# Six slots for the experts' weights, and the up product in two loops of six chunks

## The chip, the core and the metric

The kernel runs on one core of one Trainium2 chip. The metric is the device time of one execution in microseconds (us); lower is better. The core's engines are named as in the profile: PE (TensorE; PEld is its weight loads, PEldq its sequencer), DVE (VectorE), ACT (ScalarE), POOL (GpSimd) and SP (SyncE), which in this kernel issues nearly all transfers from HBM.

## The reference

`x` has 256 tokens of width 1024, in fp32. A first block of two layers (swiglu, a mixer with dilated attention and a short convolution, swiglu again) is followed by a second block: an mLSTM layer with a dense swiglu, then a state-space (S5) layer with a mixture of experts. The change touches this last part alone:

```python
def moe_ffn(u, w_router, w13, w2):
    t = u.reshape(-1, D)
    logits = t @ w_router
    top_val, top_idx = lax.top_k(logits, TOP_K)          # 2 of 8 experts
    top_w = jax.nn.softmax(top_val, axis=-1)
    for e in range(N_EXPERTS):
        gate_e = sum(where(top_idx == e, top_w, 0))
        out = out + gate_e[:, None] * swiglu(t, w13[e], w2[e])
```

`w13[e]` is 1024 x 5632 (gate and up side by side), `w2[e]` is 2816 x 1024, so an expert has 33,792 KB of weights. Each is read once.

## The kernel before

**Staging of weights.** Weights go from HBM through a ring of three slots in SBUF (`ring`, `SLOTS = 3`, 5632 fp32 columns each). SP runs through all chunks of the program in one fixed order. Before each it waits on the slot's semaphore `chunk_done`, which PE (or DVE) raises when it has finished with the slot, and the transfer raises `chunk_in`, on which PE waits (`chunk_landed`). The class `Place` works out, from a count of everything that comes earlier, which slot and which use of it a chunk has (`slot`, n % 3 and n // 3). Numbers that grow inside a hardware loop are computed in registers.

**The end of the state-space layer.** It is followed by the product `glu` (four chunks) and a layer norm, then the router: a product, the choice of two experts per token, ranks, and a count of tokens for each expert. In this stretch (2211 to 2232 us) PE, DVE and ACT hand small pieces to each other. The three slots are filled with the first chunks of expert 0 by then, and SP waits.

**The expert loop.** PE's code (`expert`, L1321) is a hardware loop over eight experts (L1379). In it `count` is loaded into a register, and an If (L1381) takes one of two bodies: `expert(e, NARROW)` where at most 88 tokens chose the expert, and, laid out behind it, `expert(e, S)` for up to 256. In the profiled execution all eight experts took the narrow body; at its end PE's sequencer jumps over the wide body to the two instructions that close the loop, and from there back to its start. A body has four steps:

- gather: the chosen tokens are picked by a product with a selection matrix (L1331, L1339); ACT and DVE copy them to `h`.
- up: `Rounds(4, (4, 4, 3), DT, "up_e")`. A hardware loop of four rounds on PE (`up_rounds`, L1298, its branch is L1303), each with three chunks of 4, 4 and 3 output tiles of 128 columns, 2048, 2048 and 1536 KB. That is 11 tiles x 8 steps of depth x 2 halves of the columns at L1314. The first two rounds are the gate's 22 tiles, which ACT takes through Silu into `mid` (L1831); the other two are the up's, which DVE multiplies into `mid` (L3068). ACT and DVE each have a hardware loop of two rounds for this. Four PSUM banks are used in turn, starting from bank 0 in each round.
- down: `Sides((0, 8, 15, 22), "down_e")`. Two halves of 512 output columns, each in three chunks of 8, 7 and 7 tiles of depth (2048, 1792 and 1792 KB), at L1358.
- scatter: the result is spread back to the tokens (L1374) and DVE adds it to `x`.

So an expert has 12 chunks of up and 6 of down, 18 in all, and each of the three slots is used six times.

**The work area.** `work` has 112 tiles of 256 columns. The experts use tiles 0 to 59 of it (`mid` 0 to 21, selections 24 to 29, the tokens `h_tok` 44 to 51, `y_pos` 52 to 59), the router's weights lie at 60, and `y_t` of `glu` at 96 to 103. The state-space layer uses nearly all of `work` until its last output has been moved (`gelu_moved`).

Of the kernel before, what the change touches and what calls it, by code (L numbers as in the profile page):

```python
# [15 lines left out]
P = 128  # L16
# [22 lines left out]
NE = 8  # L39
# [11 lines left out]

SLOTS = 3
WIDE = 2 * FT * P
BANKS = 8
# [64 lines left out]
class Rounds:  # L119
# [4 lines left out]
    def __init__(self, rounds, chunks, depth, source):  # L124
        self.rounds, self.depth, self.source = rounds, depth, source
        self.edges = [depth * sum(chunks[:c]) * P for c in range(len(chunks) + 1)]
        self.per_full, self.per_free = [0] * LIN, [0] * LIN
        self.at, n = [], 0
        for groups in chunks:
            row = []  # L130
            for m in range(groups):
                b = n % LIN
                row.append((n, b, self.per_full[b], self.per_free[b]))
                self.per_free[b] += 1
                if m < groups - 1:
                    self.per_full[b] += 1
                n += 1
            self.at.append(row)
        self.groups = n

    def counts(self):
        c = {"chunk": self.rounds * SLOTS, "of " + self.source: self.rounds}
        for b in range(LIN):
            c[f"full{b}"] = self.rounds * self.per_full[b]
            c[f"free{b}"] = self.rounds * self.per_free[b]
        return c


class Sides:
# [7 lines left out]
    def counts(self):  # L157
        return {"chunk": 2 * self.parts, "of " + self.source: 2, **{f"free{b}": 1 for b in range(LIN)}}

# [26 lines left out]
def stages():  # L186
# [90 lines left out]
class Place:  # L277


    def __init__(self, plan, name, rep=0):  # L280
        self.name, self.what, self.rep = name, plan.stage[name], rep
        self.base, self.period = plan.base[name], plan.period[name]

# [105 lines left out]
def build(nc, dram, out, periods):  # L389
    plan = Plan()  # L390
    with ExitStack() as ctx:
# [184 lines left out]
        bank_full = [signal[f"full{b}"] for b in range(BANKS)]  # L576
        chunk_in = [sem(f"chunk_in{s}") for s in range(SLOTS)]
        chunk_done = [sem(f"chunk_done{s}") for s in range(SLOTS)]
        small_in = sem("small_in")
# [46 lines left out]

        def round_end(p, c, m, i, after=0):

            n, b, k, _ = p.what.at[c][m]
            if m == len(p.what.at[c]) - 1:  # L630
                slot, use = p.slot(c, i)
                return chunk_done[slot], use + after + 2
            return bank_full[b], products(p, b, k + after * p.what.per_full[b], i, p.what.per_full[b])

# [5 lines left out]
        def _(sp):  # L640
# [20 lines left out]
            def stream_rounds(p):  # L661
                lin = p.what
                with sp.Fori(0, lin.rounds) as i:
                    src = dram[lin.source][p.of("of " + lin.source, 0, i, 1)]
                    for c, (lo, hi) in enumerate(zip(lin.edges, lin.edges[1:])):
                        slot, use = p.slot(c, i)
                        sp.wait_ge(chunk_done[slot], use + 1)
                        sp.dma_start(ring[:, slot, 0:hi - lo], src[:, lo:hi]).then_inc(chunk_in[slot], 16)

            def stream_sides(p):  # L670
                down = p.what
                for side in range(2):
                    src = dram[down.source][p.of("of " + down.source, side)]
                    for part, (lo, hi) in enumerate(zip(down.edges, down.edges[1:])):
                        slot, use = p.slot(side * down.parts + part)
                        sp.wait_ge(chunk_done[slot], use + 1)
                        sp.dma_start(ring[:, slot, 0:(hi - lo) * 512], src[:, lo * 512:hi * 512]).then_inc(chunk_in[slot], 16)

# [23 lines left out]
        def _(pe):  # L702
# [596 lines left out]
            def up_rounds(p, gp, width):  # L1299

                lin = p.what
                columns = columns_of_tile(width)
                with pe.Fori(0, lin.rounds) as i:  # L1303
                    for c, members in enumerate(lin.at):
                        slot = chunk_landed(p.slot(c, i))
                        for m, (n, b, _, k_free) in enumerate(members):
                            pe.wait_ge(bank_free[b], reads(p, b, k_free, i, lin.per_free[b]))
                            for k in range(lin.depth):
                                if c == 0 and m == 0:
                                    fb, use = gathered(k)  # L1310
                                    pe.wait_ge(bank_free[fb], reads(gp, fb, use) + 1)
                                w = ring[:, slot, (m * lin.depth + k) * P:(m * lin.depth + k + 1) * P]
                                for lo, hi in columns:
                                    mm = pe.matmul(half(b)[lo:hi, 0:width], w[:, lo:hi], h[:, k, 0:width],  # L1314
                                                   start=(k == 0), stop=(k == lin.depth - 1))
                            if m == len(members) - 1:
                                mm.then_inc(chunk_done[slot], 1)
                            else:
                                mm.then_inc(bank_full[b], 1)

            def expert(e, width):  # L1321
# [28 lines left out]
                for side in range(2):  # L1350
                    for part, (first, last) in enumerate(zip(down.edges, down.edges[1:])):
                        slot = chunk_landed(p.slot(side * down.parts + part))
                        if side == 0 and part == down.parts - 1:
                            for _, b, _, _ in late:
                                pe.wait_ge(bank_free[b], reads(p, b))
                        for n in reversed(range(lists)):
                            for k in range(first, last):
                                mm = pe.matmul(bank(2 * side + n)[0:slots(n), :],  # L1358
                                               mid[:, k, n * P:n * P + slots(n)],
                                               ring[:, slot, (k - first) * 512:(k - first + 1) * 512],  # L1360
                                               start=(k == 0), stop=(k == FT - 1))
# [37 lines left out]
        def _(act):  # L1399
# [419 lines left out]
            for e in steps.loop("expert", NE):  # L1819
# [6 lines left out]
                lin = p.what  # L1826
                with act.Fori(0, lin.rounds // 2) as i:
                    for c, members in enumerate(lin.at):
                        for m, (n, b, _, k) in enumerate(members):
                            act.wait_ge(*round_end(p, c, m, i))  # L1830
                            act.activation(mid[:, at(i, lin.groups, n), :], half(b), ACT.Silu).then_inc(bank_free[b], 1)  # L1831
                p = place("downE", e)
                for side in range(2):
                    slot, use = p.slot((side + 1) * p.what.parts - 1)
                    act.wait_ge(chunk_done[slot], use + 2)
# [12 lines left out]
        def _(dve):  # L1848
# [1201 lines left out]
            def one_expert(e, between=None):  # L3050
# [255 lines left out]
```

## Time and profile before

| | us |
|---|---|
| median of three runs | 3071.79 (3070.0 to 3074.74) |
| the profiled execution's own time | 3076.41 |
| its span in the trace | 3074.3 |
| experts, start of expert 0's products to the end of expert 7 | 2232 to 3054 |
| share of TensorE's full clock, mean | 0.991 |

The page of the profile sums each engine's busy time and idle time over the span; the rows by stretch and the timeline say where they lie. "Idle before" an instruction is put down to what released it; "issue" means that nothing the profile shows was waited for. Records of PE come in two kinds, MATMUL (PE) and LDWEIGHTS (PEld); each fp32 product has two of either. The profile's DMA part lists transfers by queue: q1 carries the weights that SP asks for, q8 carries instructions.

### The profile page before, as it was taken

To read this page: it belongs to the slowest core of one execution; us is meant where nothing else is said; L and a number is where in the kernel's file an instruction comes from. 1 tells how busy PE (TensorE), PEld (TensorE's weight loads), DVE (VectorE), ACT (ScalarE), POOL (GpSimd) and SP (SyncE) were. 2 spreads that over 40 slices of the span, in tenths; PEclk is the share of its full clock that TensorE was granted. 3 is DMA by queue.
4 is the path that set the end of the run, shared out by engine and by line. 5 is a ranking of instruction groups with operands and counts; after the bars stand their busy time and mean duration, and the time that the engine had idled before them with its cause. 6 is when DMAs were issued, how large, how long until landed. Compare 5 with 4: busy or idle time off the path is not lost.

```text
span 3074.3 us, 68427 instructions
## 1 busy us (share of the span) xinstructions
PE 2939.0 (96%) x28798; PEld 2585.7 (84%) x28799; DVE 1586.9 (52%) x3012; ACT 608.9 (20%) x1439; POOL 15.6 (1%) x27
## 2 busy tenths in 40 slices
PE   5999999999999999999999989997999999999999
PEld 4999888899999989889999779986786668766875
DVE  6776662376677667326767458899421112111212
ACT  1111104121111211412112302135212101210121
POOL 0000000000000000000000000000000000000000
PEclk9999999999999999999999999998999999999999
DMA  7665654355466565534556347832287898889885
GB/s 306 255 248 192 260 216 188 137 193 206 193 250 243 220 246 220 199 113 190 213 213 233 127 180 301 322 145 83 105 328 296 315 368 344 328 317 368 344 330 202
DMA packets 55543, 733.17 MB, mean 238 GB/s; under 512 B 6608, under 2 KB 6792, under 8 KB 10804
## 3 DMA queue, kind: packets, MB, share of 16 engines
q1 hardware_dynamic: 51364, 716.68, 59.9%
q0 software_dynamic: 3984, 13.74, 1.3%
q8 instruction: 140, 2.29, 0.3%
q14 instruction: 55, 0.45, 0.0%
HBM read 729.31 MB, written 4.23 MB: 239 GB/s over the span
## 4 chain that ended last, share of the span: by engine, by line
PE 82%; DMA 11%; DVE 5%; issue 1%; ACT 1%; SPq 0%; DVEq 0%; ACTq 0%
PE psum L728 35%; PE psum L819 17%; PE psum L1358 10%; PE psum L1314 9%; DMA ring<-in_up_e_dram 4%; PE psum L806 3%; PE psum L722 2%; DMA ring<-in_up_dram 2%; DMA ring<-in_down_e_dram 1%; PE psum L1374 1%; DMA ring<-in_w_v_dram 1%; DVE ring L1866 1%; DMA ring<-in_w_ccch_dram 1%; PE psum L1339 1%; DMA ring<-in_ada_dram 1%
## 5 line engine op out<-in xcount | busy, mean ns | idle before, releaser
L1314 PE MATMUL psum<-h_t,ring 128*64 128x88 f32 x11264 | 436.5, 239 | 16.5 <-DMA ring<-in_up_e_dram 16.1
L1314 PEld LDWEIGHTS psum<-h_t,ring 128*64 128x64 f32 x11264 | 430.2, 137 | 22.2 <-issue 21.1
L728 PE MATMUL psum<-work,ring 128*128 128x128 f32 x3680 | 440.8, 275 | 2.2 <-ACT work L1447 2.2
L728 PEld LDWEIGHTS psum<-work,ring 128*128 128x128 f32 x3680 | 425.2, 192 | 3.1 <-issue 1.6
L728 PE MATMUL psum<-work 128*128 128x128 f32 x3328 | 388.9, 275 | 2.0 <-issue 1.0
L728 PEld LDWEIGHTS psum<-work 128*128 128x128 f32 x3328 | 380.0, 192 | 2.6 <-issue 2.0
L1866 DVE SCALAR_TENSOR_TENSOR ring<-ring,cond 128x1024 f32<-128x1024 f32 x240 | 279.3, 1219 | 86.7 <-DMA ring<-in_ada_dram 86.6
L1358 PE MATMUL psum<-ring,work 128*88 128x512 f32 x704 | 304.0, 593 | 2.4 <-DMA ring<-in_down_e_dram 2.4
L819 PE MATMUL psum<-work,ring 128*128 128x256 f32 x1344 | 296.2, 383 | 4.8 <-DMA ring<-in_m_out_dram 3.1
L819 PEld LDWEIGHTS psum<-work,ring 128*128 128x128 f32 x1344 | 257.4, 192 | 42.2 <-DMA ring<-in_m_out_dram 3.9
L819 PE MATMUL psum<-h_t,ring 128*128 128x256 f32 x1280 | 278.8, 380 | 1.0 <-ACT h_t L1568 1.0
L819 PEld LDWEIGHTS psum<-h_t,ring 128*128 128x128 f32 x1280 | 242.4, 190 | 36.0 <-issue 2.8
L1358 PEld LDWEIGHTS psum<-ring,work 128*88 128x88 f32 x704 | 109.9, 157 | 190.9 <-issue 187.3
L728 PE MATMUL psum<-h_t,ring 128*128 128x128 f32 x2272 | 266.3, 275 | 4.3 <-DMA ring<-in_up_dram 3.3
L728 PEld LDWEIGHTS psum<-h_t,ring 128*128 128x128 f32 x2272 | 259.9, 192 | 6.9 <-DMA ring<-in_up_dram 4.4
L3068 DVE TENSOR_TENSOR work<-work,psum 128x256 f32 x176 | 74.1, 421 | 369.0 <-PE psum L1314 369.0
L1958 DVE TENSOR_TENSOR work<-ring 128x1024 f32<-128x1024 f32 (+1 forms) x93 | 120.0, 1291 | 144.7 <-DMA ring<-in_up_dram 77.4
L3074 DVE SCALAR_TENSOR_TENSOR x_t<-psum,mod,x_t 128x256 f32<-128x256 f32 x64 | 28.0, 483 | 293.9 <-PE psum L1374 293.9
L728 PE MATMUL psum<-h_t,work 128*128 128x128 f32 x1136 | 138.4, 275 | 0.0
L728 PEld LDWEIGHTS psum<-h_t,work 128*128 128x128 f32 x1136 | 132.6, 192 | 0.0
L806 PE MATMUL psum<-work,ring 128*128 128x257 f32 x448 | 102.9, 388 | 29.7 <-DVE work L2202 26.0
L806 PEld LDWEIGHTS psum<-work,ring 128*128 128x128 f32 x448 | 86.4, 194 | 44.8 <-issue 31.7
(378 smaller groups left out, 2538.8 us busy)
## 6 DMA issues: line engine op xcount, KB each, us to landing
ring<-in_up_e_dram SPq DMA_DIRECT2D x64, 2048.0 KB, 8.3
ring<-in_ada_dram SPq DMA_DIRECT2D x60, 2048.0 KB, 8.0
ring<-in_up_dram SPq DMA_DIRECT2D x55, 2048.0 KB, 8.7
ring<-in_down_e_dram SPq DMA_DIRECT2D x32, 1792.0 KB, 8.1
ring<-in_down_dram SPq DMA_DIRECT2D x20, 2816.0 KB, 10.3
ring<-in_up_e_dram SPq DMA_DIRECT2D x32, 1536.0 KB, 8.9
ring<-in_down_e_dram SPq DMA_DIRECT2D x16, 2048.0 KB, 8.3
ring<-in_w_qk_dram SPq DMA_DIRECT2D x12, 2048.0 KB, 8.2
```

The costliest lines, as they stand in the source:

```text
L722: mm = pe.matmul(half(bank_of), right(i), left(0, i), start=(first and i == 0), stop=(i == lin.depth - 1), skip_group_check=not first)
L728: mm = pe.matmul(bank(bank_of)[:, pair * P:(pair + 1) * P], w, right(i), start=(first and pair == 0 and i == 0), stop=(pair == lin.pairs - ...
L806: mm = pe.matmul(psum[:, b * 512:b * 512 + S + 1], ring[:, slot, (m * DT + k) * P:(m * DT + k + 1) * P], raw[:, k, :], start=(k == 0), sto ...
L819: mm = pe.matmul(half(b), w, moving(k, j * lin.groups + m), start=(k == 0), stop=(k == depth - 1))
L1314: mm = pe.matmul(half(b)[lo:hi, 0:width], w[:, lo:hi], h[:, k, 0:width], start=(k == 0), stop=(k == lin.depth - 1))
L1339: mm = pe.matmul(half(b)[lo:hi, 0:width], h_tok[:, t, f * P + lo:f * P + hi], sel[:, t, 0:width], start=(t == 0), stop=(t == TT - 1))
L1358: mm = pe.matmul(bank(2 * side + n)[0:slots(n), :], mid[:, k, n * P:n * P + slots(n)], ring[:, slot, (k - first) * 512:(k - first + 1) * 512],
L1374: mm = pe.matmul(half(b), y_pos[0:slots(n), n, f * P:(f + 1) * P], gate_sel[0:slots(n), n, :], start=(n == 0), stop=(n == lists - 1))
L1866: e = dve.scalar_tensor_tensor(w, w, 1.0, cond[:, :], ALU.mult, ALU.mult, accum_out=col)
L1958: dve.tensor_tensor(s1, a21, a22, ALU.add).then_inc(signal["weight_sums"], 1)
L3068: dve.tensor_tensor(o, o, half(b), ALU.mult).then_inc(bank_free[b], 1)
L3074: dve.scalar_tensor_tensor(x[:, f, :], half(b), mod1[:, 5 * DT + f:5 * DT + f + 1], x[:, f, :], ALU.mult, ALU.add).then_inc(bank_free[b], 1)
```

## The change

`DEEP` is 6. Slots 0 to 2 remain the ring's, slots 3 to 5 are three stretches of the work area, tiles 60 to 107. Only the experts' chunks go round all six (`deep`), so each slot is used three times in an expert. SP's order is unchanged: glu's four chunks, then expert 0's. SP may fill slots 3 to 5 for the first time when DVE has raised their `chunk_done`, which it does right after `gelu_moved`. To make room, `y_t` moves to tiles 36 to 43 and the router's weights to 108. A round of up now has six chunks, (4, 4, 3, 4, 4, 3), and there are two rounds: the first is the whole gate, the second the whole up. PE keeps a hardware loop, now over two rounds with a body of 22 tiles, in the narrow and in the wide body alike. ACT's and DVE's loops over rounds are gone; their 22 instructions stand one behind the other. SP computes the source's address for each chunk and not once for a round.

```diff
 SLOTS = 3
+DEEP = 2 * SLOTS
...
-        self.edges = [depth * sum(chunks[:c]) * P for c in range(len(chunks) + 1)]
+        self.per_row = len(chunks) // 2
+        starts = [sum(chunks[c - c % self.per_row:c]) for c in range(len(chunks))]
+        self.edges = [(c // self.per_row, depth * n * P, depth * (n + many) * P) for c, (n, many) in enumerate(zip(starts, chunks))]
...
-        "upE": Rounds(4, (4, 4, 3), DT, "up_e"), "downE": Sides((0, 8, 15, 22), "down_e"),
+        "upE": Rounds(2, (4, 4, 3, 4, 4, 3), DT, "up_e"), "downE": Sides((0, 8, 15, 22), "down_e"),
...
+    def deep(self, pos, i=0):
+
+        pos += DEEP * 2 if self.name == "downE" else 0
+        n = self.plan.base["upE"]["chunk"] + pos % DEEP
+        slot, use = (n % SLOTS, n // SLOTS) if pos % DEEP < SLOTS else (pos % DEEP, 0)
+        use += pos // DEEP
+        for reg, per in ((self.rep, SLOTS), (i, 1)):
+            if isinstance(reg, int):
+                use = use + reg * per
+            else:
+                use = reg * per + use
+        return slot, use
...
-        y_t = tiles(96, DT)
+        y_t = tiles(36, DT)
...
-        w_router = flat(60, 1)[:, 0:DT * NE].rearrange("p (k n) -> p k n", n=NE)
+        w_router = flat(108, 1)[:, 0:DT * NE].rearrange("p (k n) -> p k n", n=NE)
+
+        deep_slot = [ring[:, n, :] for n in range(SLOTS)] + [flat(60 + 16 * n, 16) for n in range(SLOTS)]
...
                 with sp.Fori(0, lin.rounds) as i:
-                    src = dram[lin.source][p.of("of " + lin.source, 0, i, 1)]
-                    for c, (lo, hi) in enumerate(zip(lin.edges, lin.edges[1:])):
-                        slot, use = p.slot(c, i)
+                    for c, (part, lo, hi) in enumerate(lin.edges):
+                        src = dram[lin.source][p.of("of " + lin.source, part, i, 2)]
+                        slot, use = p.deep(c, i)
                         sp.wait_ge(chunk_done[slot], use + 1)
-                        sp.dma_start(ring[:, slot, 0:hi - lo], src[:, lo:hi]).then_inc(chunk_in[slot], 16)
+                        sp.dma_start(deep_slot[slot][:, 0:hi - lo], src[:, lo:hi]).then_inc(chunk_in[slot], 16)
...
                 with pe.Fori(0, lin.rounds) as i:
                     for c, members in enumerate(lin.at):
-                        slot = chunk_landed(p.slot(c, i))
+                        slot = chunk_landed(p.deep(c, i))
...
-                                w = ring[:, slot, (m * lin.depth + k) * P:(m * lin.depth + k + 1) * P]
+                                w = deep_slot[slot][:, (m * lin.depth + k) * P:(m * lin.depth + k + 1) * P]
...
-                with act.Fori(0, lin.rounds // 2) as i:
-                    for c, members in enumerate(lin.at):
-                        for m, (n, b, _, k) in enumerate(members):
-                            act.wait_ge(*round_end(p, c, m, i))
-                            act.activation(mid[:, at(i, lin.groups, n), :], half(b), ACT.Silu).then_inc(bank_free[b], 1)
+                for c, members in enumerate(lin.at):
+                    for m, (n, b, _, k) in enumerate(members):
+                        act.wait_ge(*round_end(p, c, m, 0))
+                        act.activation(mid[:, n, :], half(b), ACT.Silu).then_inc(bank_free[b], 1)
...
             dve.sem_inc(signal["gelu_moved"], 1)
+            for slot in range(SLOTS, DEEP):
+                dve.sem_inc(chunk_done[slot], 1)
...
-                for i in steps.loop("upE rounds", lin.rounds // 2):
-                    for c, members in enumerate(lin.at):
-                        for m, (n, b, _, k) in enumerate(members):
-                            dve.wait_ge(*round_end(p, c, m, i, lin.rounds // 2))
-                            o = mid[:, at(i, lin.groups, n), :]
-                            dve.tensor_tensor(o, o, half(b), ALU.mult).then_inc(bank_free[b], 1)
+                for c, members in enumerate(lin.at):
+                    for m, (n, b, _, k) in enumerate(members):
+                        dve.wait_ge(*round_end(p, c, m, 1))
+                        dve.tensor_tensor(mid[:, n, :], mid[:, n, :], half(b), ALU.mult).then_inc(bank_free[b], 1)
```

## Rows read from the trace of the kernel before

**Rows 1.** The page, part 1: busy time, share of the span, instructions.
```profile
PE 2939.0 (96%) x28798; PEld 2585.7 (84%) x28799; DVE 1586.9 (52%) x3012; ACT 608.9 (20%) x1439; POOL 15.6 (1%) x27
```

**Rows 2.** Busy time by stretch, experts 0 to 2 (columns in the first line).
```profile
core 0: us, PE busy (x) PEld busy (x) DVE busy (x) ACT busy (x) POOL busy (x), PEclk, DMA share, GB/s
...
2232.00:2333.20 101.20, 98.68 (x1577) 72.97 (x1576) 21.16 (x55) 15.80 (x33) 0.00 (x0) 1.00 0.85 334
2333.20:2442.30 109.10, 100.71 (x1579) 75.06 (x1578) 16.49 (x41) 15.78 (x33) 0.00 (x0) 0.97 0.80 318
2442.30:2544.40 102.10, 98.95 (x1578) 73.24 (x1578) 16.45 (x41) 15.79 (x33) 0.00 (x0) 1.00 0.86 339
```

**Rows 3.** Waits from 2232 to 3054 us: us in total, times, longest.
```profile
PE psum L1314 <- DMA ring<-in_up_e_dram: 16.1, 24, 1.3
...
PE psum L1358 <- DMA ring<-in_down_e_dram: 2.4, 5, 0.8
```

**Rows 4.** DMA from 2232 to 2333 us: GB/s in 40 slices, then issues.
```profile
GB/s 0 6 0 149 428 383 428 384 446 409 409 324 441 409 440 326 422 389 402 436 378 425 372 406 403 414 128 318 422 290 437 177 380 267 182 428 324 337 389 248
...
ring<-in_up_e_dram SPq DMA_DIRECT2D x8, 2048.0 KB, 8.5
```

**Rows 5.** Timeline of PE, 2248 to 2284 us: start, us, what, idle before.
```profile
2263.18 13.57 PE L1314 MATMUL psum<-h_t,ring 128*64 128x88 f32 x352 [0.40 <-DMA ring<-in_up_e_dram]
```

**Rows 6.** DMA queues by packets, 2210 to 2232 us: packets, MB, share.
```profile
q8 instruction: 2, 0.03, 0.5%
```

**Rows 7.** DMA queues, 2232 to 2345 us.
```profile
q8 instruction: 6, 0.10, 0.4%
```

**Rows 8.** DMA queues, 2333 to 2345 us, from the end of expert 0 on.
```profile
q8 instruction: 2, 0.03, 0.9%
```

**Rows 9.** DMA queues, 2345 to 3050 us: q1, with the line that follows it.
```profile
q1 hardware_dynamic: 17712, 236.46, 85.2%
issues: line engine op xcount, KB each, median us to landing
```

**Rows 10.** DMA queues, 820 to 1600 us, the second pass of the layer loop.
```profile
q8 instruction: 48, 0.79, 0.4%
```

**Rows 11.** The page, part 3: the same queue over the whole execution.
```profile
q8 instruction: 140, 2.29, 0.3%
```

**Rows 12.** Busy time by stretch, 820 to 1600 us (columns as in rows 2).
```profile
820.00:1600.00 780.00, 771.29 (x5854) 732.16 (x5853) 482.35 (x852) 149.57 (x401) 3.22 (x4) 1.00 0.55 208
```

**Rows 13.** Branches of PE's sequencer, line 1381: ns min/median/max.
```profile
L1381 PEldq COMPARE_BRANCH  x16: 76/129/5902, 2230.8 to 3052.7; - x16
```

**Rows 14.** The same, line 964, the layer loop's branch.
```profile
L964 PEldq COMPARE_BRANCH  x2: 82/1864/3646, 812.7 to 1589.4; - x2
```

**Rows 15.** The same, line 1303, the loop of up.
```profile
L1303 PEldq COMPARE_BRANCH  x32: 76/208/257, 2247.2 to 3011.7; - x32
```

**Rows 16.** The same, line 1379, the loop of experts.
```profile
L1379 PEldq COMPARE_BRANCH  x8: 76/208/238, 2338.2 to 3053.0; - x8
```

**Rows 17.** The page, part 5: groups of up and down.
```profile
L1314 PE MATMUL psum<-h_t,ring 128*64 128x88 f32 x11264 | 436.5, 239 | 16.5 <-DMA ring<-in_up_e_dram 16.1
...
L1358 PE MATMUL psum<-ring,work 128*88 128x512 f32 x704 | 304.0, 593 | 2.4 <-DMA ring<-in_down_e_dram 2.4
...
L3068 DVE TENSOR_TENSOR work<-work,psum 128x256 f32 x176 | 74.1, 421 | 369.0 <-PE psum L1314 369.0
```

**Rows 18.** Line 1339, and what it does.
```profile
L1339 PE MATMUL psum<-work x512: 239/239/409, 2231.9 to 2955.4; 128*64 128x88 f32 x171
```

**Rows 19.** Line 1374.
```profile
L1374 PE MATMUL psum<-work x128: 377/379/382, 2329.6 to 3053.5; 88*128 88x256 f32 x128
```

**Rows 20.** Timeline of PE around 2339 us.
```profile
2339.61 0.68 PE L1331 MATMUL psum<-ident,work 128*128 128x128 f32 x2 [6.41 <-issue]
```

**Rows 21.** Timeline of PE around 2443 us.
```profile
2442.88 0.43 PE L1331 MATMUL psum<-ident,work 128*128 128x128 f32 x2 [0.60 <-issue]
```

**Rows 22.** The chain of waits, 2232 to 2250 us: start, us, what.
```profile
2234.58 13.50 PE psum L1314 x352
```

More of the change, by code:

```diff
@@ L141, in counts @@
     def counts(self):
-        c = {"chunk": self.rounds * SLOTS, "of " + self.source: self.rounds}
+        c = {"chunk": self.rounds * SLOTS, "of " + self.source: 2 * self.rounds}
         for b in range(LIN):
@@ L157, in counts @@
     def counts(self):
-        return {"chunk": 2 * self.parts, "of " + self.source: 2, **{f"free{b}": 1 for b in range(LIN)}}
+        return {"chunk": SLOTS, "of " + self.source: 2, **{f"free{b}": 1 for b in range(LIN)}}
 class Made:
@@ L281, in __init__ @@
         self.name, self.what, self.rep = name, plan.stage[name], rep
[L282 removed]
+        self.plan, self.base, self.period = plan, plan.base[name], plan.period[name]
     def of(self, signal, k=0, i=0, per=0):
@@ L576, in build @@
         bank_full = [signal[f"full{b}"] for b in range(BANKS)]
-        chunk_in = [sem(f"chunk_in{s}") for s in range(SLOTS)]
-        chunk_done = [sem(f"chunk_done{s}") for s in range(SLOTS)]
+        chunk_in = [sem(f"chunk_in{s}") for s in range(DEEP)]
+        chunk_done = [sem(f"chunk_done{s}") for s in range(DEEP)]
         small_in = sem("small_in")
@@ L619, in group_end, with round_end @@
             return bank_full[b], products(p, b, k, i, 0 if isinstance(i, int) else p.what.per_full[b])
-        def round_end(p, c, m, i, after=0):
+        def round_end(p, c, m, i):
             n, b, k, _ = p.what.at[c][m]
             if m == len(p.what.at[c]) - 1:
-                slot, use = p.slot(c, i)
-                return chunk_done[slot], use + after + 2
-            return bank_full[b], products(p, b, k + after * p.what.per_full[b], i, p.what.per_full[b])
+                slot, use = p.deep(c, i)
+                return chunk_done[slot], use + 2
+            return bank_full[b], products(p, b, k, i, p.what.per_full[b])
         def gathered(f):
@@ L674, in stream_sides @@
                     for part, (lo, hi) in enumerate(zip(down.edges, down.edges[1:])):
-                        slot, use = p.slot(side * down.parts + part)
+                        slot, use = p.deep(side * down.parts + part)
                         sp.wait_ge(chunk_done[slot], use + 1)
-                        sp.dma_start(ring[:, slot, 0:(hi - lo) * 512], src[:, lo * 512:hi * 512]).then_inc(chunk_in[slot], 16)
+                        sp.dma_start(deep_slot[slot][:, 0:(hi - lo) * 512], src[:, lo * 512:hi * 512]).then_inc(chunk_in[slot], 16)
             for part, times in stages():
@@ L1351, in expert @@
                     for part, (first, last) in enumerate(zip(down.edges, down.edges[1:])):
-                        slot = chunk_landed(p.slot(side * down.parts + part))
+                        slot = chunk_landed(p.deep(side * down.parts + part))
                         if side == 0 and part == down.parts - 1:
@@ L1359, in expert @@
                                                mid[:, k, n * P:n * P + slots(n)],
-                                               ring[:, slot, (k - first) * 512:(k - first + 1) * 512],
+                                               deep_slot[slot][:, (k - first) * 512:(k - first + 1) * 512],
                                                start=(k == 0), stop=(k == FT - 1))
@@ L1826, in _ @@
                 lin = p.what
-                with act.Fori(0, lin.rounds // 2) as i:
-                    for c, members in enumerate(lin.at):
-                        for m, (n, b, _, k) in enumerate(members):
-                            act.wait_ge(*round_end(p, c, m, i))
-                            act.activation(mid[:, at(i, lin.groups, n), :], half(b), ACT.Silu).then_inc(bank_free[b], 1)
+                for c, members in enumerate(lin.at):
+                    for m, (n, b, _, k) in enumerate(members):
+                        act.wait_ge(*round_end(p, c, m, 0))
+                        act.activation(mid[:, n, :], half(b), ACT.Silu).then_inc(bank_free[b], 1)
                 p = place("downE", e)
                 for side in range(2):
-                    slot, use = p.slot((side + 1) * p.what.parts - 1)
+                    slot, use = p.deep((side + 1) * p.what.parts - 1)
                     act.wait_ge(chunk_done[slot], use + 2)
```

2 lines of the change are left out of this document (1 added, 1 removed).

## The prediction

> **What bounds the kernel now.** I read the page's first part, then busy time by stretch, then what PE waits for among the experts, and last the queue that carries instructions. PE is busy for 2939.0 us of 3074.3 [rows 1]; the change can only give back its idle time. An expert takes 102.1 us, of which PE is busy 98.95 [rows 2]. Of the idle time among all experts, 16.1 us in 24 waits is PE at up waiting for a chunk, and 2.4 us in 5 waits at down [rows 3]; each is short. One stands in the timeline: 0.40 us of idle before a round of 13.57 us [rows 5]. The rate is near what the transfers reach: the slices show 324 to 448 GB/s through up [rows 4], where a round asks for 5632 KB in 13.57 us, or 425 GB/s [rows 5].
>
> The row that matters more is another. q8 carries instructions, in packets of 16 KB (0.79 MB in 48) [rows 10]. Two packets come in the 21 us ahead of the experts, six in the 113 us of expert 0 and the start of expert 1 [rows 6, 7], and in the 705 us after that none: behind q1's line the list of queues ends [rows 9]. So PE's sequencer holds the code of the narrow body, and runs it seven times without a fetch. In the second pass of the layer loop every instruction has been run before, and yet 48 packets come [rows 10]: code of that length isn't held.
>
> How much code is a packet? The second pass has 5854 + 5853 records of PE and PEld [rows 12]; over 48 that is 244 to a packet, the rest being waits and register steps. A trip through the narrow body: one round of up 11264 / 32 = 352 products and as many loads [rows 17] (PE and PEld have equal counts [rows 1]), 704; down 88 and 88 [rows 17]; gather 64 and 64 [rows 18], and 4 of the transposes [rows 20]; scatter 16 and 16 [rows 19]. Together 1044, or 4.3 packets.
>
> What does it cost when code isn't there? PE's jump at L1381 over the wide body takes 5902 ns the first time, and 129 at the median [rows 13]. PE stood idle for 6.41 us [rows 20], where the next expert shows 0.60 [rows 21]. The layer loop's jump back, also to code not held, takes 3646 ns [rows 14], in a part of the kernel whose transfers average 208 GB/s [rows 12] and not 339 [rows 2]. Jumps to code that is held take 208 ns at the median, back to the start of a round or of an expert [rows 15, 16].
>
> **The change part by part.** The sum is made against the profiled execution's 3076.4 us (span 3074.3); the median shown is 4.6 us lower.
>
> *Waits for chunks.* With six slots a chunk is asked for up to five chunks ahead of its use. The mean demand, 339 GB/s [rows 2], stays below the 380 to 448 that most slices show [rows 4], and down takes 304 / 8 = 38 us [rows 17] for a third of the bytes, in which six slots fill up. All 18.5 us go: -18.5 (bounds: -18.5 and 0).
>
> *First loads.* Slots 3 to 5 are filled in the router stretch, where SP waits today and q1 is idle but for its first microseconds; nothing there waits for a large transfer. 0. It is hidden behind small pieces of DVE and PE; without that cover three chunks would take some 15 us (6 MB at the rates of rows 4).
>
> *ACT, DVE, SP.* ACT and DVE are busy some 16 us of an expert's 102 [rows 2]; a loop less changes nothing. Six address computations on SP lie ahead of transfers that are early. The banks' order has a wait at down for the tile before the last, which DVE has by then multiplied: it takes 0.42 us [rows 17], while the last tile's products take 13.57 / 11 = 1.2. 0, and at most 0.5 us for an expert if DVE were late, 4 us in all.
>
> *PE's code.* Up's body doubles: 1044 + 704 = 1748 records, 7.2 packets. The wide body behind it grows too, so the code that closes the expert loop lies farther off. One trip now touches eight packets of the body; the fetch runs one ahead (the jump at the end of expert 0 brings two packets, not one [rows 8]), so nine; with the two at the jump's target, eleven. Before, the same count gave eight (two and six [rows 6, 7]), and eight were held. Nothing shows that more are. What is held lies between 8 and 47 packets; I take the nearest row, eight. If the oldest go first, a round of eleven through a store of eight finds none of its next ones: both jumps of each expert miss, and all packets come again.
>
> The Trainium skill, in "Runtime: NRT & Kernel Launch", section "Instruction fetch mechanics", gives TensorE an instruction memory of 128 KiB, refilled in blocks of 16 KiB; that is eight blocks, and the block's size agrees with q8's packets here. The same section also says that only two blocks are a window and that a jump outside them stalls. By that, 32 jumps back to the start of a round of 2.9 packets would have missed in this trace; their median of 208 ns speaks against it [rows 15]. The measurement decides: more than two are held.
>
> Costs of the misses, each counted less the 0.2 us of a jump that hits:
> - The jump over the wide body: expert 0 pays it today; seven more. It comes while the last chunks of the refill are running, as today: 7 x 5.7 = +40 (low 7 x 3.4 = 24, if it meets quiet queues).
> - The jump back to the loop's start, missed seven times. It follows the first by 6 us, when six slots are full and transfers have ended, as at the layer loop: 7 x 3.4 = +24 (high 7 x 5.7 = 40).
> - Straight code at up's pace: 704 records in 13.5 us is 52 per us, so a packet lasts 4.7 us. In expert 0 the first round ran at that pace from fresh code in 13.50 us against 13.57 for a held one [rows 5, 22], so it cost nothing, but transfers had barely begun (0, 6, 0 and 149 GB/s in the first four slices [rows 4]). Under full traffic a fetch can take the 5.9 us of the jump, 1.2 us too long. Six such packets in seven experts: 0 to 50 us. I take 3 us for an expert, +21.
> - Up's own jump back stays a hit: its body is 1408 / 244 = 5.8 packets, seven blocks at most, one ahead is eight. It is made once for an expert where it was made three times; PE's queue covers it (13.57 us for a round, jump included). 0.
>
> Sum: -18.5 + 40 + 24 + 21 = +66.5, so 3142.9 for such an execution and **3138 us** against the median. With the low ends +29.5, 3101; with the high ends -18.5 + 40 + 40 + 50 = +111.5, 3183. PE ends up bound by its own fetches; what is late next is nothing, since chunks will be waiting.
>
> **The rivals.**
> - *The code fits.* The store holds eleven packets or more. For it: no row shows its upper end short of 48. Against it: nothing but the missing row. Then only the 18.5 us go: 3053. It decides at eleven packets held. This is the case on the other side.
> - *Up's jump back misses too*, if one of the eight is given up for the fetch ahead. Then each expert has one more miss and streams up's body twice: 8 x (3.4 + 3) = 51 more, 3189; to 3205 with dear misses.
> - *The deeper ring doesn't do what it says*: the code fits and PE waits on as before because the rate itself, 425 GB/s asked in up, is the limit. Against it: the mean demand. 3072.
>
> **How the numbers follow.** What this kernel's measurement can tell from no change is 0.2%, 6 us. The forecast 0.78, the code fits 0.10, up's jump misses as well 0.08, no gain and no loss 0.04. The forecast's own range is 3101 to 3183; with the second rival's and some slack at both ends, 3092 to 3205, which leaves out the two cases without misses and little more. Faster: 0.11, from the first rival and a part of the third. Slower: 0.86. The same: 0.03.
>
> **What would show it.** PE's waits for chunks under 2 us in all. At L1381 nine of sixteen jumps or so hit and eight take 3 to 6 us; at L1379 seven of eight take over 3 us; at L1303 all stay at 0.2. Nine to eleven packets on q8 for each expert, so 140 [rows 11] grows to some 220. Experts of 109 to 115 us, with 8 to 10 us of idle time at the transposes of L1331. If instead q8 shows 145 packets and experts take 100 us, the store was larger and I am wrong on the sign. If L1381 stalls but L1379 doesn't, the oldest aren't the first to go.

## The result, and the profile after

The changed kernel takes 3155.5 us (median of 4 runs, 3152.1 to 3157.8) against 3073.3 us for the kernel before (four runs by now, 3070.0 to 3074.9). The ratio is 1.0268, with a 95% interval of 1.025 to 1.0286: 82 us slower, where 66 were forecast. The profiled executions are 3152.1 and 3076.4 us, 76 us apart, and it is these that the views compare.

The page of the changed kernel, parts 1, 3 and 5, answers to [rows 1, 11, 17]. Up is now L1332.

```profile
PE 2947.8 (94%) x28798; PEld 2597.1 (82%) x28799; DVE 1586.7 (50%) x3012; ACT 600.4 (19%) x1431; POOL 15.6 (0%) x27
...
q8 instruction: 211, 3.46, 0.4%
...
L1332 PE MATMUL psum<-h_t,work 128*64 128x88 f32 x5632 | 223.4, 239 | 20.7 <-issue 20.7
```

PE's busy time is up by 9 us, its span by 76. q8 went from 140 packets [rows 11] to 211. The largest group of up has 20.7 us of idle time ahead of it, put down to "issue" and no longer to a transfer. By stretch, experts 0, 1 and 2, against [rows 2]:

```profile
2226.80:2328.00 101.20, 98.30 (x1577) 73.08 (x1576) 21.19 (x55) 14.73 (x32) 0.00 (x0) 1.00 0.86 335
2328.00:2441.40 113.40, 100.49 (x1578) 74.85 (x1578) 16.41 (x41) 14.74 (x32) 0.00 (x0) 0.95 0.78 307
2441.40:2554.50 113.10, 99.97 (x1578) 74.50 (x1578) 16.90 (x42) 14.74 (x32) 0.00 (x0) 0.95 0.79 312
```

Expert 0 takes 101.2 us in both kernels. From expert 1 on an expert takes 113 us and not 102. The third column from the end is the granted clock: 0.95 of full speed where it was 1.00. What PE waits for among the experts (L1349 is the transposes with which an expert begins, L1332 up, L875 the layer norm after the last expert), against [rows 3]:

```profile
PE psum L1349 <- issue: 74.5, 7, 10.9
...
PE psum L1332 <- issue: 20.7, 20, 2.1
...
PE psum L875 <- issue: 2.6, 1, 2.6
```

No wait for a chunk is left. In the place of 18.5 us of them stand 74.5 us ahead of the transposes of experts 1 to 7 and 20.7 us within up (2.9 of these in expert 0, which saves about as much in waits for chunks). In the kernel before, the wait ahead of the transposes (L1331) was:

```profile
PE psum L1331 <- issue: 9.8, 7, 6.4
```

The branches of PE's sequencer show what the 74.5 are. A miss is from here on a jump to code that isn't held, a hit one to code that is. First the jump over the wide body (L1399, before [rows 13]):

```profile
L1399 PEldq COMPARE_BRANCH  x16: 80/1685/5941, 2225.6 to 3124.1; - x16
```

The line has two branches for each expert, one that enters the body and is cheap, one that leaves it. Eight of the sixteen are slow, seven between 5.6 and 5.9 us and the last 3.3. The branch back to the start of the loop of experts (L1397, before [rows 16]), of which seven are taken:

```profile
L1397 PEldq COMPARE_BRANCH  x8: 79/4580/4951, 2333.0 to 3127.6; - x8
```

and up's own branch (L1321, before [rows 15]), which never misses:

```profile
L1321 PEldq COMPARE_BRANCH  x16: 76/156/256, 2258.9 to 3083.1; - x16
```

The chain of waits over the start of expert 1, start and duration in us, before [rows 20, 21]:

```profile
2327.98 10.74 issue
2338.72 0.68 PE psum L1349 x2
2339.41 4.04 PE psum L1357 x64
2343.45 16.07 PE psum L1332 x422
2359.52 0.55 issue
...
2365.13 0.87 issue
...
2371.07 0.74 issue
```

After 10.74 us of nothing the transposes and the gather run slower than before: 0.68 and 4.04 us against 0.43 and 2.58 for a gather at full clock. The granted clock was at 1.2 and not 2.4 GHz by then, as this stretch of the busy times shows (0.50). It begins 4.2 us into the pause and ends 3.7 us into the work:

```profile
2332.20:2342.40 10.20, 3.68 (x44) 3.35 (x46) 0.82 (x2) 0.77 (x2) 0.00 (x0) 0.50 0.03 5
```

Then, in the first pass over up's body, three pauses of 0.5 to 0.9 us. The second pass (28.18 us, 734 records) has none. Transfers on q8 in one expert (2441 to 2554 us), where the kernel before shows none [rows 9]:

```profile
q1 hardware_dynamic: 2637, 35.16, 78.5%
q8 instruction: 10, 0.16, 0.7%
```

Summed over the experts, from the first gather product to the end of the last scatter, the trace has 898.4 us against 821.9, 76.5 more: idle time at the transposes 74.5 - 9.8 = +64.7 (6.4 of the 9.8 are the one slow jump of before [rows 20]), pauses in up +20.5, waits for chunks -18.5, gather products 32.4 - 22.5 = +9.9 and transposes +1.5 at the lower clock. That is 78.1; 1.6 us of it are not placed. Behind the experts the last jump costs 2.6 us more, and the layer norm that follows it 1.7 us, again at the lower clock (its first products in the chain of waits, start and duration). Before:

```profile
3053.87 3.47 PE psum L857 x16
```

and after:

```profile
3127.88 5.19 PE psum L875 x16
```

Together that is 80.8 us. The part ahead of the experts happened to be 5.1 us shorter in this execution, which leaves the 76 of the spans.

### The profile page after: what moved, and what is told of

The parts are those of the page before. It is cut to its first block, busy times and chain, and to the rows that moved or that the text cites. A ratio compares the mean times of both kernels' runs of the same rounds, so it can differ in the third digit from the quotient of the medians.

```text
span 3150.1 us, 67796 instructions
## 1 busy us (share of the span) xinstructions
PE 2947.8 (94%) x28798; PEld 2597.1 (82%) x28799; DVE 1586.7 (50%) x3012; ACT 600.4 (19%) x1431; POOL 15.6 (0%) x27
## 4 chain that ended last, share of the span: by engine, by line
PE 86%; DVE 5%; DMA 5%; issue 4%; ACT 1%; SPq 0%; DVEq 0%; ACTq 0%
PE psum L746 34%; PE psum L837 17%; PE psum L1332 14%; PE psum L1376 10%; PE psum L824 3%; PE psum L740 2%; DMA ring<-in_up_dram 1%; DMA ring<-in_w_ccch_dram 1%; PE psum L1357 1%; PE psum L1392 1%; DVE ring L1883 1%; DMA ring<-in_ada_dram 1%; DMA ring<-in_m_out_dram 1%; PE psum L939 1%; DVE work L1869 1%
## 5 line engine op out<-in xcount | busy, mean ns | idle before, releaser
L746 PEld LDWEIGHTS psum<-work,ring 128*128 128x128 f32 x3680 | 425.2, 192 | 3.1 <-issue 1.6
L837 PEld LDWEIGHTS psum<-work,ring 128*128 128x128 f32 x1344 | 256.2, 191 | 43.1 <-DMA ring<-in_m_out_dram 5.1
L3085 DVE TENSOR_TENSOR work<-work,psum 128x256 f32<-128x256 f32 x176 | 74.1, 421 | 371.3 <-PE psum L1332 371.3
L1332 PE MATMUL psum<-h_t,work 128*64 128x88 f32 x5632 | 223.4, 239 | 20.7 <-issue 20.7
L1332 PEld LDWEIGHTS psum<-h_t,work 128*64 128x64 f32 x5632 | 218.0, 137 | 24.5 <-issue 24.5
L1332 PE MATMUL psum<-h_t,ring 128*64 128x88 f32 x5632 | 217.2, 239 | 0.0
L1332 PEld LDWEIGHTS psum<-h_t,ring 128*64 128x64 f32 x5632 | 215.2, 137 | 0.1
L1376 PE MATMUL psum<-ring,work 128*88 128x512 f32 x352 | 152.9, 594 | 0.0
L1376 PE MATMUL psum<-work 128*88 128x512 f32 x352 | 152.4, 592 | 0.0
L1376 PEld LDWEIGHTS psum<-work 128*88 128x88 f32 x352 | 55.3, 157 | 95.8 <-issue 95.8
## 6 DMA issues: line engine op xcount, KB each, us to landing
ring<-in_down_dram SPq DMA_DIRECT2D x20, 2816.0 KB, 10.5
work<-in_down_e_dram SPq DMA_DIRECT2D x16, 1792.0 KB, 10.2
```

The costliest lines, as they stand in the source:

```text
L746: mm = pe.matmul(bank(bank_of)[:, pair * P:(pair + 1) * P], w, right(i), start=(first and pair == 0 and i == 0), stop=(pair == lin.pairs - ...
L837: mm = pe.matmul(half(b), w, moving(k, j * lin.groups + m), start=(k == 0), stop=(k == depth - 1))
L1376: mm = pe.matmul(bank(2 * side + n)[0:slots(n), :], mid[:, k, n * P:n * P + slots(n)], deep_slot[slot][:, (k - first) * 512:(k - first + 1 ...
L3085: dve.tensor_tensor(mid[:, n, :], mid[:, n, :], half(b), ALU.mult).then_inc(bank_free[b], 1)
```

## The experiments

**e1: the longer code alone.** The kernel before, three slots, with PE's loop of up over pairs of rounds:

```diff
-                with pe.Fori(0, lin.rounds) as i:
-                    for c, members in enumerate(lin.at):
+                with pe.Fori(0, lin.rounds // 2) as pair:
+                    for i, c, members in [(at(pair, 2, r), c, members) for r in range(2) for c, members in enumerate(lin.at)]:
```

> The kernel before with its three slots and its chunks, but PE's loop of up written as two passes over a body of two rounds (22 tiles), narrow and wide. Only PE's code is longer; nothing of the six slots is in it. Theory (PE's sequencer holds eight packets of code, the oldest go first): the misses of the changed kernel are all there, the jump at the end of the narrow body over 5 us and the jump back to the loop's start over 4 us in each expert, q8 near 211 packets; waits for chunks stay in part, as three slots still run dry in up. 3155 to 3174 us. Rival (the loss comes from the slots in the work area or from SP's other order): no misses, 142 packets on q8, 3070 to 3076 us.

3192.3 us (3185.0 to 3194.6), ratio 1.0389 (1.0374 to 1.0405), 214 packets on q8. Waits of PE among the experts, then one expert's stretch:

```profile
PE psum L1331 <- issue: 74.2, 7, 10.9
...
PE psum L1314 <- issue: 21.0, 20, 2.0
PE psum L1314 <- DMA ring<-in_up_e_dram: 15.0, 16, 2.1
...
PE psum L1358 <- DMA ring<-in_down_e_dram: 3.9, 4, 1.9
```

```profile
2452.70:2570.00 117.30, 102.08 (x1580) 75.70 (x1578) 16.59 (x42) 15.79 (x33) 0.00 (x0) 0.94 0.77 297
```

The misses and the pauses are the changed kernel's to within 0.3 us, without one of its slots. So the code is what costs, and the slots gain: the changed kernel is 37 us faster than this one. My range ended at 3174. 18.9 us of the 37 are the waits for chunks that are left, which I had thought half hidden. PE's busy time among the experts is 9 us longer too (102.1 us in the expert shown against 100.0); a part of that is the clock (0.94 against 0.95), the rest is not placed.

**e2: no wide body.** The changed kernel, with its loop of experts cut to the narrow body:

```diff
-                many = pe.value_load(count[0:1, bass.ds(e, 1)], min_val=0, max_val=S)
-                with pe.If(many <= NARROW):
-                    expert(e, NARROW)
-                with pe.Else():
-                    expert(e, S)
+                expert(e, NARROW)
```

> The changed kernel without its wide body, and without the load of the count and the If (no expert has more than 88 tokens with these inputs). The narrow body is as long as in the changed kernel and ends in the eighth packet, but the two instructions that close the loop now stand right behind it. Theory: the long jump forward is gone with its 5.7 us for each expert; the fetch that runs ahead brings a ninth packet, so the jump back still misses (about 5 us) and all code comes again. 3155 - 7 x 6 = 3113, range 3100 to 3125, some 200 packets on q8. Rival (any body that doesn't change place, once it has been run, is held; only the far jump evicts): all hits, 3050 to 3060. Second rival (the length doesn't matter, the loss is in the slots): 3150 or more.

3086.2 us (3078.4 to 3096.3), ratio 1.0050 (1.0034 to 1.0066), 167 packets: faster than I said. The only branch left, back to the start of the loop:

```profile
L1397 PEldq COMPARE_BRANCH  x8: 78/222/6962, 2335.2 to 3054.7; - x8
```

Three of the seven miss, at 6.3 to 7.0 us: those after experts 1, 3 and 5. Experts 1, 2 and 3 by stretch, and q8 in the first two of them:

```profile
2335.50:2433.20 97.70, 97.70 (x1579) 72.97 (x1578) 16.30 (x40) 14.70 (x32) 0.00 (x0) 1.00 0.89 354
2433.20:2541.50 108.30, 100.21 (x1580) 74.55 (x1579) 16.45 (x41) 14.70 (x32) 0.00 (x0) 0.97 0.82 321
2541.50:2639.40 97.90, 97.90 (x1580) 73.12 (x1579) 16.50 (x42) 14.70 (x32) 0.00 (x0) 1.00 0.88 354
```

```profile
q1 hardware_dynamic: 2590, 34.58, 88.5%
q14 instruction: 1, 0.01, 0.0%
issues: line engine op xcount, KB each, median us to landing
```

```profile
q1 hardware_dynamic: 2591, 34.59, 81.2%
q8 instruction: 9, 0.15, 0.5%
```

Expert 1 fetches nothing and is over in 97.7 us; then the jump misses, expert 2 fetches its whole code again and takes 108; expert 3 is held again. Neither theory had this. A miss at the jump means that the start of the loop was put out for a ninth packet. The count bears that out: each miss comes with nine packets, the eight of the body and one just ahead of them, and 140 + 3 x 9 = 167; a hit brings none. Why the ninth was asked for only every second time, e10 takes up.

**e3: 96 instructions less.** As e2, and

```diff
-                        for lo, hi in columns_of_tile(width):
+                        for lo, hi in ((0, P),):
...
-                                for lo, hi in columns:
+                                for lo, hi in columns if n < lin.groups - 1 else ((0, P),):
```

> The kernel of e2 with 96 instructions less on PE, some 5% of the narrow body: the gather products and the last tile of up are made with all 128 columns in one product and not in two halves. The body then ends in the seventh packet, and with the one ahead eight are touched. Theory (eight packets held): no miss at all after expert 0, 145 packets or fewer on q8, experts of 99.5 to 100.5 us, 3052 to 3060 us, 55 us below e2. Rival (what is held is fewer than eight, or not decided by a count of packets): the jump back still misses, 3100 to 3125.

3059.4 us (3056.0 to 3066.7), ratio 0.9957 (0.9940 to 0.9973). The branch back, and q8 on the page:

```profile
L1397 PEldq COMPARE_BRANCH  x8: 67/209/231, 2334.8 to 3035.8; - x8
```

```profile
q8 instruction: 140, 2.29, 0.3%
```

No branch misses, and q8 is back at 140. An expert takes 100.1 us. A twentieth less code turns three misses into none. It is 27 us below e2 where 55 were expected, as e2 itself missed less. The shorter code isn't free: e2's experts whose code was held take 97.8 us.

**e4: six slots with the short code.** From the changed kernel: `"upE": Rounds(4, (2, 2, 2, 2, 2, 1), DT, "up_e")`, six chunks in a round of 11 tiles, and in `deep` the counts that go with it:

```diff
-        pos += DEEP * 2 if self.name == "downE" else 0
+        rounds = self.plan.stage["upE"].rounds
+        pos += DEEP * rounds if self.name == "downE" else 0
...
-        for reg, per in ((self.rep, SLOTS), (i, 1)):
+        for reg, per in ((self.rep, rounds + 1), (i, 1)):
```

ACT and DVE take their two rounds each one behind the other, without a loop.

> Six slots as in the changed kernel, wide body and If kept, but up in four rounds of 11 tiles on PE again, each round in six chunks of 2, 2, 2, 2, 2 and 1 tiles (1024 KB, the last 512), so that a chunk's slot is fixed in the code and PE's code is as long as before the change (one instruction more). Theory: the code is held as before, 141 to 144 packets on q8, and with five chunks of 1 MB asked for ahead PE's waits for chunks fall from 18.5 us to under 6: 3055 to 3062 us. Rival (small transfers cost more than they hide, or six slots don't help): 3068 to 3080. The code theory fails if it is over 3100.

**3050.1 us** (3044.9 to 3051.6), ratio 0.9920 (0.9907 to 0.9934): the fastest of all, 24 us under the kernel before, 105 under the changed one and 5 under my range, and it keeps the wide body. Experts 2 and 3, the branch at the end of the body, q8:

```profile
2434.00:2533.00 99.00, 98.41 (x1580) 73.25 (x1579) 16.54 (x41) 14.71 (x32) 0.00 (x0) 1.00 0.86 350
2533.00:2632.00 99.00, 98.42 (x1580) 73.15 (x1579) 16.55 (x42) 14.70 (x32) 0.00 (x0) 1.00 0.86 350
```

```profile
L1401 PEldq COMPARE_BRANCH  x16: 76/126/3802, 2230.2 to 3026.6; - x16
```

```profile
q8 instruction: 140, 2.29, 0.3%
```

One slow branch, as before the change; PE busy for 98.4 of 99.0 us; no wait for a chunk.

**e5: the small chunks with three slots.** The kernel before with e4's chunks, each slot used twice in a round.

> The kernel before with its three slots, but a round of up in six chunks of 2, 2, 2, 2, 2 and 1 tiles, as in e4. It parts the two things that e4 changes, slots and the chunks' size. If six slots make e4's gain: three slots then hold 3 MB and not 5.6, only 2 MB are asked for ahead, and PE waits more for chunks than the 18.5 us before: 3085 to 3130 us. If the chunks' size makes it: 3050 to 3060. No misses either way (one instruction more on PE than before, 142 packets on q8).

3196.0 us (3191.1 to 3205.7), ratio 1.0393 (1.0368 to 1.0418), no misses (140 packets). PE's waits for chunks:

```profile
PE psum L1314 <- DMA ring<-in_up_e_dram: 80.1, 83, 2.0
...
PE psum L1358 <- DMA ring<-in_down_e_dram: 31.3, 8, 4.1
```

111 us of them against 18.5, and worse than my range. That is 93 of the 128 us by which the experts are longer in the trace; the rest is PE's busy time (830 us against 793), at a mean clock of 0.97 and not 1.00. e4's gain is the slots', and small chunks alone lose 122 us, more than the changed kernel's 82, by another way. That two transfers of 1 MB in flight don't keep the rate up is my reading; no run varies it alone.

**e6: quiet queues.** The changed kernel with `src[:, lo:lo + P]` in the place of `src[:, lo:hi]`, and the like for down.

> The changed kernel with each of the experts' transfers cut to its first 128 columns (64 KB), so that q1 is nearly idle among the experts; most weights are thereby left unloaded and the experts' results are not the reference's. PE's code and its misses are the changed kernel's. Theory (the fetches of code wait behind the weights' packets): the jump forward falls from 5.7 to about 3.5 us, the jump back from 4.6 to 3.5, and the straight code of up streams without idle time (20.7 us in the changed kernel, under 4 here): 3155 - 7 x 3.3 - 18 = 3114, range 3100 to 3125, still 211 packets on q8. Rival (a fetch takes what it takes, whatever the queues do): jumps of 5.7 and 4.6 us, 20 us of idle time in up, 3150 to 3156.

3118.8 us (3116.8 to 3120.8), ratio 1.0147 (1.0120 to 1.0175), 218 packets. The jump forward, the jump back, and the two groups of up:

```profile
L1399 PEldq COMPARE_BRANCH  x16: 76/1860/4157, 2225.6 to 3088.0; - x16
```

```profile
L1397 PEldq COMPARE_BRANCH  x8: 79/4686/4773, 2327.2 to 3092.1; - x8
```

```profile
L1332 PE MATMUL psum<-h_t,ring 128*64 128x88 f32 x5632 | 216.8, 239 | 0.3
L1332 PE MATMUL psum<-h_t,work 128*64 128x88 f32 x5632 | 216.5, 239 | 0.0
```

The pauses in up are gone (0.3 us), and the jump forward takes 3.6 to 4.2 us: the weights' traffic makes the one and lengthens the other. The jump back does not follow: 4.6 to 4.8 us, as under traffic. It comes right on the heels of another miss, whose second packet is still being brought (on q8 it starts 0.4 to 0.5 us ahead of the packet that the jump back needs, and takes 1.0 to 1.4 us). That this is the cause is argued, but it fits e10: where no other jump goes before it, the jump back takes 3.8 to 4.3 us.

**e7: a twin of e3 with three slots**, which was to price the slots.

```diff
-                                for lo, hi in columns:
+                                for lo, hi in columns if n < lin.groups - 1 or k % 2 else ((0, P),):
```

> The twin of e3 with three slots: the kernel before without its wide body and If, with the gather products and as many products of up as in e3 made with all 128 columns. Against e3 it shows what the six slots are worth at the chunks' old size with the code held: e3 should be 18 to 22 us faster, so 3077 to 3081 us here, with 18 us of waits for chunks. Rival (six slots give less, and e4's gain is the small chunks'): 3062 to 3068.

3100.8 us (3096.4 to 3105.6), ratio 1.0094 (1.0072 to 1.0116). It doesn't measure what it should. One expert:

```profile
2438.00:2543.50 105.50, 105.06 (x1515) 77.26 (x1515) 16.48 (x41) 15.80 (x34) 0.00 (x0) 1.00 0.86 328
```

PE is busy for 105.1 us, against 100.1 in e3 with as many products. Here the last tile of a round alternates between a product over 128 columns and one in two halves, four times; in e3 a tile is of one kind throughout. I take that for the 5 us an expert, which hide the waits. Inconclusive on the slots; e9 replaces it.

**e8: the long body where nobody runs.** PE's loop body doubled as in e1, but for the wide body only (`many = 1 if width <= NARROW else 2` rounds to a pass).

> The kernel before with the doubled body of up in the wide body alone, which no expert runs. The jump forward at the end of the narrow body goes some 360 instructions farther, and the narrow body is as it was. Theory (what counts is how many packets a trip touches, five and one ahead and two at the target): no change, 3070 to 3077 us, 141 to 143 packets on q8, one slow jump of 3.5 to 6 us. Rival (the distance of the jump decides): the jump forward misses in each expert, 3110 to 3125.

3074.3 us (3064.4 to 3080.3), ratio 0.9996 (0.9983 to 1.0009), 139 packets. The jump forward:

```profile
L1382 PEldq COMPARE_BRANCH  x16: 76/126/5884, 2230.6 to 3052.6; - x16
```

It is slow once. How far a jump goes is nothing; how much is run between two visits decides.

**e9: three slots without the wide body**, the kernel before with e2's cut and nothing more.

> The kernel before without its wide body and If, and nothing else changed: three slots, the old chunks, products in halves. In e7 products of both widths in turn made PE itself slower, so that it was no measure of the slots. An expert should take 101 us here (102.1 less the load of the count and the If, about 1 us), against 97.8 us for those experts of e2 whose code was held: then six slots are worth 3 us an expert at the old chunks' size, as in e4 (102.1 to 98.9). 3062 to 3068 us, no misses. Rival (e2's 97.8 owes most to the missing If): 98 us here, 3040 us.

3063.5 us (3059.7 to 3074.3), ratio 0.9981 (0.9968 to 0.9993). Two experts:

```profile
2432.80:2533.60 100.80, 98.67 (x1579) 73.29 (x1578) 16.44 (x41) 15.75 (x33) 0.00 (x0) 1.00 0.87 343
2634.20:2735.50 101.30, 98.87 (x1580) 73.39 (x1579) 16.52 (x41) 15.84 (x34) 0.00 (x0) 1.00 0.87 342
```

100.8 to 101.3 us (101.2 as the mean of experts 1 to 7), against 97.7 to 97.9 for e2's held experts: with the code held, six slots are worth 3.1 to 3.4 us an expert at the old chunks' size, some 26 us in all. 20.7 us of it are e9's waits for chunks; e2 has none. e4 gives the same, 102.1 to 99.0.

**e10: e2 with quiet queues.**

> e2 (six slots, doubled body, no wide body) with the experts' transfers cut to 64 KB each as in e6; the experts' results are again not the reference's. In e2 the jump back missed in every second expert alone. Theory (an expert that runs fresh code is late with its fetches, so the one that would bring a ninth packet has not begun when it jumps back; one whose code is held makes that fetch in time and loses the loop's start): with quiet queues no fetch is late, and the jump back misses in all seven experts, 4 to 5 us each, 3085 to 3095 us and some 190 packets on q8. Rival (the alternation belongs to the order in which packets are replaced): misses in every second expert here too, 3 or 4 of them, 3065 to 3075 us, 165 packets.

3066.3 us (3056.1 to 3077.7), ratio 0.9986 (0.9968 to 1.0004), 185 packets. The branch back:

```profile
L1397 PEldq COMPARE_BRANCH  x8: 78/3830/4275, 2335.6 to 3046.4; - x8
```

Five of seven miss (3.8 to 4.3 us), those after experts 0 and 3 don't. The packets are again nine for a miss, 140 + 5 x 9 = 185. Misses and packets lie between the two expectations, the time lies in the rival's range, as a miss costs less here. The misses don't alternate, which is against the rival; not every jump misses, which is against the theory. Five misses against e2's three would fit a race between the fetch of the ninth packet and the jump, but that is not shown: each count is of one execution, e2's profiled run is the fastest of its six (3078.4 to 3096.3 us), and at some 10 us for a miss (108.3 against 97.7) the others can have had one or two more. What decides a single one stays open.

## Why the prediction was right

**The code is no longer held, and both jumps miss.** Right, and it was the whole of the sign. The prediction took the least store that [rows 6, 7, 9] allow, eight packets. e1 shows the misses without the slots, e8 that distance doesn't count, and e2, e3 and e10 set the edge: a trip that with the fetch ahead can touch nine packets misses whenever the ninth is brought (three and five times of seven), and one that touches eight never does. That eight was exactly the size is in part luck, as the rows allowed anything up to 47. The Trainium skill gives the same eight in "Runtime: NRT & Kernel Launch", section "Instruction fetch mechanics" (128 KiB in blocks of 16); e3 bears that out. That section's window of two blocks doesn't hold here: in e3 a trip of seven packets never stalls. One trip of the changed kernel fetches ten packets, not eleven: the eighth packet's own fetch ahead isn't made in this execution. In e1 it is made at the end of three experts (214 packets), with quiet queues (e6) at the end of seven of the eight (218).

**The sizes.** Jumps: 40 + 24 = 64 us forecast, 64.7 + 2.6 = 67.3 found, with two errors that nearly cancel. The seventh of the added jumps forward, behind the last expert, costs 2.6 us and not 5.7, as no weights are on their way any more; the jump back takes 4.6 us and not 3.6, seven times. Straight code: 21 forecast, 20.5 found; e6 shows that the weights' traffic makes it. The 21 was picked between 0 and 50, so that it fits to half a microsecond is luck. Chunks: -18.5 both. Up's own jump stays a hit, as said; the second rival is out.

**What was missing.** The step that was mis-sized is the sum of the misses, which priced PE's idle time and not what it does to the clock: after 10.7 us of idle time the gather runs at 1.2 GHz, +11.4 us among the experts and +1.7 in the layer norm behind them. With 3.3 us more for the jumps that is 16.4 us; less the 1.6 us that aren't placed it makes the 80.8 us of the trace out of the 66.5 forecast, to within half a microsecond. The medians are 82.2 us apart, 1.4 more, which is within what single executions differ by. The kernel before showed this price in one row, at the one miss that it had: its L1339 has a largest product of 409 ns against a median of 239 [rows 18], and [rows 2] a clock of 0.97 for that expert. Two readings of the prediction are off without weight: the slices of [rows 4] reach 446 GB/s and not 448, and of the 32 branches of [rows 15] 24 jump back, the last of each expert's four doesn't.

**The rivals.** "The code fits" would have given 3053; e3 and e4, whose code does fit, take 3059 and 3050. The sum without misses was right, the case wasn't. "The deeper ring doesn't do what it says" is refuted by e4, and by e2 against e9. First loads, SP's order, ACT and DVE at nothing: expert 0, which has all of these and no slow jump before it, takes 101.2 us in both, with 2.9 us of pauses for code in the place of 2.2 us of waits for chunks.

## What to carry to other kernels

Count the code of a hardware loop as one counts SBUF: a trip's distinct packets (16 KB each, some 244 records of PE and PEld), with the one fetched ahead and the two at each far jump, against the eight that TensorE's sequencer held here. A deeper ring of buffers doesn't need a longer unrolled body. Let the chunks of one round fill all slots (e4), and keep the body. Where a page shows instruction packets inside a loop that has been run before, look there ahead of any wait for data.

## What the runs showed of the hardware

- A jump to code that isn't held takes 3.3 to 4.3 us with quiet queues (e6, e10, the last of the changed kernel) or with less than 1 MB of weights still to come (e4 3.8, e5 4.2), and 5.4 to 7.0 us while the last 1.3 to 1.4 MB of a refill of the slots come in (before, after, e1, e2); a second one right behind it takes 4.5 to 5.0 us in both.
- Code run in a straight line at 52 instructions per us keeps up with its own fetches when the queues are quiet, and pauses for 0.2 to 2.1 us at a packet's edge under traffic, 20.7 us over eight experts.
- Around a pause of PE of 10.5 to 10.9 us the granted clock stands at half for 10.2 to 13.7 us, from 1.9 to 4.5 us into the pause until 3.2 to 6.2 us into the work behind it (the changed kernel's experts 1 to 7). With quiet queues it is the same: pauses of some 9 us in e6, 10.2 us at half clock each.
- Sixteen products over 128 columns an expert, taken in turn with products in two halves of 64, go with 105.1 us of PE's busy time (e7); the same number in two whole tiles with 100.1 (e3). The two kernels differ in their slots and rounds too, so the cause is argued and not shown.
- A loop whose trip can touch nine packets misses in some trips and not in others: three of seven in e2, five in e10, one execution each. Each miss brings all nine.
